# Down weights loaded as pairs of neighbouring rows per partition, activations transposed with a stride of two

## The chip, the core and the metric

The kernel runs on one core of one Trainium2 chip. A time is the device time of one execution in microseconds (us). The kernel before was timed in three runs: median 1532.12 us, from 1531.06 to 1533.81.

## The reference

A two-layer decoder trunk on 256 tokens of width 1024, in float32. The parts that the change touches are the two feed-forward blocks; both are SwiGLU, and the second one is applied once per expert with a gate per token.

```
# layer 0: x += diff_attention(rmsnorm(x));  x += swiglu(rmsnorm(x), wg, wu, wd)      (D_FF = 2816)
# layer 1: x += rglru_block(rmsnorm(x));     x += moe_swiglu(rmsnorm(x), ...)         (8 experts, top 2, D_FF_EXPERT = 3584)
def swiglu(t, wg, wu, wd):
    return (jax.nn.silu(t @ wg) * (t @ wu)) @ wd

def moe_swiglu(h, router, wg, wu, wd):
    ...
    for e in range(N_EXPERTS):
        out = out + comb[:, e:e + 1].astype(t.dtype) * swiglu(t, wg[e], wu[e], wd[e])
```

In `t @ wd` the contraction runs over the hidden width (2816 or 3584). The result does not depend on the order in which the hidden columns are taken, as long as activation and weight take the same one.

## The kernel before

All weights go through one stream of pieces of 1 MB (128 partitions x 2048 floats). SyncE issues them in program order (`load`, L312 to L316). Each landing slot is written again only after the piece that lay in it has been worked off: ring of 4 slots (`w_ring`) up to the experts, of 7 (three more in `work`) for the experts. For each piece ScalarE writes a rounded copy `w_hi` (L396), VectorE the remainder `w_lo` = piece - `w_hi` (L696, in the experts L1071), and TensorE multiplies with both: three fp32r matmuls (hi x hi, lo x hi, hi x lo) for each tile (`mm3`, L1157). `w_hi` and `w_lo` have 4 slots, freed by TensorE (`piece_used`).

The dense FFN works in chunks of 512 hidden columns (five, and one of 256), the experts in 7 chunks of 512. A chunk is gate, up, silu x up, a transpose of the activation by TensorE, and the product with the down weights one chunk later. A gate or up piece (`cols4`) has 4 runs of 512 floats per partition, which is 2 KB each. A down piece is 256 rows of the down weight: in the dense FFN `rows2` puts row r0 + p and row r0 + 128 + p on partition p, two runs of 4 KB; in the experts the view `md` does the same. The activation is turned in blocks of 128 neighbouring columns: `turn_chunk` (L1327) turns 4 blocks for each of two token blocks, `turn_e` (L1474) turns 4 blocks. In such a transpose the activation block is the stationary operand (loaded by LDWEIGHTS, engine PEld) and the identity the moving one. Block s, partition p then holds hidden column 128 s + p, and meets weight half s of the piece.

One expert pass is 42 pieces: 28 of gate and up, 14 of down. For each such piece TensorE runs 12 matmuls of 512 columns, in the dense FFN 24. The profiled execution made 8 passes. Its order of work is written out by hand for every engine, and nothing is scheduled by costs. At the end of a pass TensorE gathers the tokens of the next expert (L1428) and, at the start of the next, scatters the results (L1437, L1438).

Of the kernel before, what the change touches and what calls it, by code (L numbers as in the profile page):

```python
# [2 lines left out]

# [13 lines left out]
P = 128  # L29
# [11 lines left out]
def build_trunk(nc, x, norm_mix, norm_ffn, norm_final, rel_bias, w_qkv, w_o, lq1, lk1, lq2, lk2, subln,  # L41
# [16 lines left out]
    CW = 512  # L58
    EC = FE // CW
    FC = FF // CW  # L60
# [8 lines left out]
    def cols4(w, half, c0):  # L69
        return w.rearrange("(c p) n -> p c n", p=P)[:, 4 * half:4 * half + 4, c0:c0 + 512]  # L70

    def cols8(w, c0):
        return w.rearrange("(c p) n -> p c n", p=P)[:, :, c0:c0 + 256]

    def rows2(w, r0):
        return w[r0:r0 + 256, :].rearrange("(s p) n -> p s n", p=P)

    static = []
    wq = w_qkv[0]
    for part in range(2):  # L80
# [6 lines left out]
    fg, fu, fd = f_gate[0], f_up[0], f_down[0]  # L87
    for i in range(FC):
        static += [cols4(fg, h, CW * i) for h in range(2)]
        if i:  # L90
            static += [rows2(fd, CW * (i - 1) + 256 * h) for h in range(2)]
        static += [cols4(fu, h, CW * i) for h in range(2)]
    static += [cols8(fg, CW * FC)] + [rows2(fd, CW * (FC - 1) + 256 * h) for h in range(2)]
    static += [cols8(fu, CW * FC), rows2(fd, CW * FC)]

    def f_gate_at(i):
        return P_FFN + (0 if i == 0 else 6 * i - 2)
# [32 lines left out]
    def half_slot(n):  # L130
        return HALF[(n - P_MOE) % PASS]
# [3 lines left out]

    mg = m_gate.rearrange("a e (c p) f -> (a e) p c f", p=P)
    mu = m_up.rearrange("a e (c p) f -> (a e) p c f", p=P)
    md = m_down.rearrange("a e (s p) n -> (a e) p s n", p=P)

    def expert_pieces(e):  # L140
        pieces = []
        for i in range(EC):
            pieces += [mg[e, :, 4 * h:4 * h + 4, CW * i:CW * i + CW] for h in range(2)]
            pieces += [mu[e, :, 4 * h:4 * h + 4, CW * i:CW * i + CW] for h in range(2)]
            if i:
                pieces += [md[e, :, 4 * (i - 1) + 2 * h:4 * (i - 1) + 2 * h + 2, :] for h in range(2)]
        pieces += [md[e, :, 4 * (EC - 1) + 2 * h:4 * (EC - 1) + 2 * h + 2, :] for h in range(2)]
        return pieces

    def at(i):  # L150
        return 0 if i == 0 else 4 + 6 * (i - 1)
# [3 lines left out]
    with ExitStack() as ctx:  # L155
        def sb(name, shape, dt=F32):
            return ctx.enter_context(nc.sbuf_tensor(name, shape, dt))
# [14 lines left out]
        ident = sb("ident", [P, P])  # L172
# [56 lines left out]
        act_f = work[:, 0:1024].rearrange("p (b n) -> p b n", b=NB)  # L229
# [16 lines left out]
        act_e = work[:, 0:512]  # L246
# [19 lines left out]
        ps = ctx.enter_context(nc.psum_tensor("ps", [P, 8, 512], F32))  # L266
        GB, UB, TB, SB_, M0, M1, D0, D1 = range(8)
# [881 lines left out]
        def _(pe):  # L1149
            T = nc.tensor  # L1150

            def mm3(acc, xh, xl, wh, wl, start, stop, weights_stay=False):

                terms = ((xh, wh), (xl, wh), (xh, wl))
                for k, (a, b) in enumerate(terms):
                    stationary, moving = (b, a) if weights_stay else (a, b)
                    ins = T.matmul(acc, stationary, moving, start=start and k == 0, stop=stop and k == 2)  # L1157
                return ins
# [100 lines left out]
            for k in range(4):  # L1259
                ins = T.matmul(ps[:, 4 + k, :], flip, bias_up[:, 512 * k:512 * k + 512], start=True, stop=True)  # L1260
# [59 lines left out]
            transpose_hn(range(4), 0, norm=1)  # L1320
            pe.wait_ge(xt_lo_ok, 10)

            def turn_chunk(i, subs):
                for b in range(NB):
                    pe.wait_ge(fa, 2 * i + b + 1)
                    for s in range(subs):
                        ins = T.transpose(ps[:, 2 + b, P * s:P * s + P], act_f[:, b, P * s:P * s + P], ident[:, :])  # L1327
                    ins.then_inc(ft, 1)

            def narrow(n, banks):  # L1330
# [74 lines left out]
            for b in range(NB):  # L1405
                for c in range(KC):
                    ins = T.matmul(ps[:, M0, E * b:E * b + E], xtf[:, c, P * b:P * b + P], rw[:, c, :],
                                   start=c == 0, stop=c == KC - 1)
# [23 lines left out]
            def scatter():  # L1432

                for k, bank in enumerate((M0, M1, SB_, TB)):
                    b, half = divmod(k, 2)
                    o = slice(512 * half, 512 * half + 512)
                    T.matmul(ps[:, bank, :], onehotT[:, P * b:P * b + P], y_hi[:, o], start=True, stop=False)  # L1437
                    T.matmul(ps[:, bank, :], onehotT[:, P * b:P * b + P], y_lo[:, o], start=False,  # L1438
                             stop=True).then_inc(sc_ps, 1)
# [8 lines left out]
            def expert(p):  # L1448
                def slot(j):
                    n = P_MOE + j  # L1450
                    pe.wait_ge(lo_ready, p * PASS + (n + 1))
                    return w_hi[:, half_slot(n), :], w_lo[:, half_slot(n), :]

                def up_or_gate(j, bank, half):
                    wh, wl = (w.rearrange("p (c n) -> p c n", c=4) for w in slot(j))
                    for c in range(4):
                        ins = mm3(ps[:, bank, :], xt_hi[:, 4 * half + c, 0:P], xt_lo[:, 4 * half + c, 0:P],
                                  wh[:, c, :], wl[:, c, :], half == 0 and c == 0, half == 1 and c == 3)
                    ins.then_inc(piece_used, 1)

                def down_e(j, i, h):
                    wh, wl = (w.rearrange("p (s n) -> p s n", s=2) for w in slot(j))
                    for s in range(2):
                        for half, bank in enumerate((D0, D1)):
                            o = slice(512 * half, 512 * half + 512)
                            ins = mm3(ps[:, bank, :], eT_hi[i % 2][:, 2 * h + s, :], eT_lo[i % 2][:, 2 * h + s, :],
                                      wh[:, s, o], wl[:, s, o], (i, h, s) == (0, 0, 0), (i, h, s) == (EC - 1, 1, 1))
                    ins.then_inc(piece_used, 1)

                def turn_e(i):  # L1470
                    pe.wait_ge(ea_ok, p * EC + (i + 2))
                    pe.wait_ge(el_ok, p * EC + (i + 1))
                    for s in range(4):
                        ins = T.transpose(ps[:, TB, P * s:P * s + P], act_e[:, P * s:P * s + P], ident[:, :])  # L1474
                    ins.then_inc(et_ps, 1)

                for i in range(EC):
                    g0 = at(i)
                    pe.wait_ge(es_ok, p * EC + (i + 1))
                    if i == 0:  # L1480
                        pe.wait_ge(gat_hi, p * 2 + 2)
                        pe.wait_ge(gat_lo, p * 2 + 2)
                    up_or_gate(g0, GB, 0)
                    up_or_gate(g0 + 1, GB, 1)
                    if i == 0:
                        pe.wait_ge(ys_lo, p + 1)
                        pe.wait_ge(oht_ok, p + 1)
                        pe.wait_ge(el_ok, p * EC + 1)
                        scatter()
                    else:  # L1490
                        if i == 1:
                            pe.wait_ge(sc_ok, p * 4 + 4)
                            pe.wait_ge(oh_ok, p * 2 + 2)
                        turn_e(i - 1)
                        if i == 1:
                            for b in range(NB):
                                ins = T.transpose(ps[:, SB_, P * b:P * b + P], onehot[:, b, :].bitcast(F32), ident[:, :])
                            ins.then_inc(oht_ps, 1)
                    pe.wait_ge(ea_ok, p * EC + (i + 1))
                    up_or_gate(g0 + 2, UB, 0)  # L1500
                    up_or_gate(g0 + 3, UB, 1)
                    if i == EC - 1:
                        pe.wait_ge(oh_ok, p * 2 + 4)
                        pe.wait_ge(oht_ok, p + 2)
                        pe.wait_ge(es_ok, p * EC + (EC + 1))
                        gather(range(4))
                    if i:
                        pe.wait_ge(el_ok, p * EC + (i + 1))
                        down_e(g0 + 4, i - 1, 0)
                        if i == EC - 1:  # L1510
                            turn_e(i)
                        down_e(g0 + 5, i - 1, 1)
                pe.wait_ge(el_ok, p * EC + (EC + 1))
                down_e(PASS - 2, EC - 1, 0)
                down_e(PASS - 1, EC - 1, 1)
# [37 lines left out]
```

## Time and profile before

| | before |
|---|---|
| median of three runs | 1532.12 us |
| profiled execution, span | 1531.7 us |
| TensorE matmul busy | 1452.7 us (95%) |
| VectorE busy | 1164.9 us (76%) |
| ScalarE busy | 938.2 us (61%) |
| DMA, whole span | 427.41 MB in 193388 packets |

The span runs from the first to the last instruction of the core in the profiled execution; the page gives no other time of it. PE is the matmul side of TensorE and PEld its weight load; they overlap. A matmul's record contains its latency, so single records overlap and their means are longer than the pace at which they follow each other. The pace is read from the chain of waits. The expert passes lie between about 500 and 1520 us.

### The profile page before, as it was taken

What the parts mean: (1) busy time and instruction counts of PE and PEld (TensorE: products, weight loads), DVE (VectorE), ACT (ScalarE), POOL (GpSimd) and SP (SyncE); (2) the same over time, 40 slices, a digit from 0 to 9 for tenths busy, and PEclk for the clock granted to TensorE, in tenths of its full rate; (3) what the DMA queues carried; (4) which work ended last, traced back from release to release, by engine and by line L of the source; (5) the groups of instructions that cost most, each with busy time, mean ns of one, the idle gap of its engine ahead of it and who ended that gap; (6) DMA issues with size and microseconds to landing.
All of it is one profiled execution on the core that took longest, in us unless ns stands there. A gap on an engine that the chain in (4) does not pass through costs nothing.

```text
span 1531.7 us, 19136 instructions
## 1 busy us (share of the span) xinstructions
PE 1452.7 (95%) x7099; PEld 1215.4 (79%) x7099; DVE 1164.9 (76%) x1047; ACT 938.2 (61%) x778; POOL 11.6 (1%) x30
## 2 busy tenths in 40 slices
PE   5988999999989999999999999999999999999996
PEld 5877788888977778778878877877887887787785
DVE  5667444537675899888879788887888978888786
ACT  4554434434843677667667667766776766776674
POOL 3000000000000000000000000000000000000000
PEclk9998999999998999999999999999999999999999
DMA  9434345662462899899899989989989998998991
GB/s 280 154 110 155 127 172 192 210 222 84 151 242 86 304 335 369 313 352 370 316 333 387 342 329 351 362 313 340 365 311 350 385 344 328 350 363 310 337 370 48
DMA packets 193388, 427.41 MB, mean 279 GB/s; under 512 B 6921, under 2 KB 30049, under 8 KB 193345
## 3 DMA queue, kind: packets, MB, share of 16 engines
q1 hardware_dynamic: 192560, 425.49, 76.6%
q0 software_dynamic: 784, 1.33, 0.5%
q8 instruction: 29, 0.48, 0.1%
q14 instruction: 15, 0.11, 0.0%
HBM read 425.73 MB, written 1.06 MB: 279 GB/s over the span
## 4 chain that ended last, share of the span: by engine, by line
PE 83%; DVE 10%; issue 3%; ACT 3%; DMA 1%; DVEq 0%; SPq 0%; ACTq 0%
PE ps L1157 76%; DVE w_lo L1071 5%; PE ps L1428 2%; PE ps L1474 1%; ACT w_hi L396 1%; DVE w_lo L696 1%; DMA w_ring<-in_attn_w_qkv_dram 1%; PE ps L1211 1%; DVE hn L716 1%; PE ps L1437 1%; PE ps L1438 1%; DVE xres L782 0%; PE ps L1377 0%; DVE work L952 0%; DVE xt_lo L1076 0%
## 5 line engine op out<-in xcount | busy, mean ns | idle before, releaser
L396 ACT ACTIVATE w_hi<-w_ring 128x2048 fp32r<-128x2048 f32 x256 | 486.3, 1915 | 234.4 <-PE ps L1157 224.1
L1157 PE MATMUL ps<-w_hi,xt_hi 128*128 128x512 f32 (+1 forms) x1344 | 535.4, 398 | 28.7 <-DVE xt_lo L1076 18.3
L1157 PE MATMUL ps<-w_lo,xt_hi 128*128 128x512 f32 (+1 forms) x1344 | 525.7, 391 | 0.0
L1157 PE MATMUL ps<-w_hi,xt_lo 128*128 128x512 f32 (+1 forms) x1344 | 525.5, 391 | 0.0
L1071 DVE TENSOR_TENSOR w_lo<-w_ring,w_hi 128x2048 fp32r<-128x2048 f32 x191 | 432.3, 2286 | 65.4 <-ACT w_hi L396 65.0
L1071 DVE TENSOR_TENSOR w_lo<-work,w_hi 128x2048 fp32r<-128x2048 f32 x141 | 320.3, 2287 | 50.1 <-ACT w_hi L396 50.1
L396 ACT ACTIVATE w_hi<-work 128x2048 fp32r<-128x2048 f32 x144 | 275.2, 1917 | 108.8 <-PE ps L1157 108.4
L1157 PEld LDWEIGHTS ps<-w_hi,xt_hi 128*128 128x128 f32 x1344 | 255.7, 190 | 86.1 <-DVE w_lo L1071 25.1
L1157 PEld LDWEIGHTS ps<-w_lo,xt_hi 128*128 128x128 f32 x1344 | 255.9, 190 | 54.2
L1157 PEld LDWEIGHTS ps<-w_hi,xt_lo 128*128 128x128 f32 x1344 | 256.4, 191 | 50.3 <-issue 0.2
L1157 PE MATMUL ps<-w_hi,split 128*128 128x512 f32 x768 | 239.1, 393 | 9.2 <-DVE split L962 4.1
L696 DVE TENSOR_TENSOR w_lo<-w_ring,w_hi 128x2048 fp32r<-128x2048 f32 x65 | 148.1, 2287 | 65.2 <-ACT w_hi L396 65.1
L1157 PEld LDWEIGHTS ps<-w_hi,split 128*128 128x128 f32 x768 | 143.8, 189 | 43.1 <-DVE w_lo L1071 5.2
L1157 PE MATMUL ps<-w_lo,split 128*128 128x512 f32 x384 | 150.0, 390 | 0.0
L396 ACT ACTIVATE split<-ps 128x512 fp32r<-128x512 f32 (+2 forms) x53 | 34.1, 653 | 113.4 <-PE ps L1327 50.0
L1157 PE MATMUL ps<-xt_hi,w_hi 128*128 128x256 f32 x288 | 84.4, 293 | 7.7 <-DVE xt_lo L722 4.9
L1157 PEld LDWEIGHTS ps<-w_lo,split 128*128 128x128 f32 x384 | 72.4, 189 | 15.4
L1157 PE MATMUL ps<-xt_lo,w_hi 128*128 128x256 f32 x288 | 82.6, 287 | 0.0
L1157 PE MATMUL ps<-xt_hi,w_lo 128*128 128x256 f32 x288 | 82.5, 287 | 0.0
L1157 PEld LDWEIGHTS ps<-xt_hi,w_hi 128*128 128x128 f32 x288 | 56.4, 196 | 8.8 <-DVE xt_lo L722 4.2
L1157 PEld LDWEIGHTS ps<-xt_lo,w_hi 128*128 128x128 f32 x288 | 56.5, 196 | 0.1
L1157 PEld LDWEIGHTS ps<-xt_hi,w_lo 128*128 128x128 f32 x288 | 56.4, 196 | 0.0
(226 smaller groups left out, 808.7 us busy)
## 6 DMA issues: line engine op xcount, KB each, us to landing
w_ring<-in_moe_w_up_dram SPq DMA_DIRECT2D x72, 1024.0 KB, 7.0
w_ring<-in_moe_w_down_dram SPq DMA_DIRECT2D x72, 1024.0 KB, 7.1
work<-in_moe_w_gate_dram SPq DMA_DIRECT2D x64, 1024.0 KB, 6.5
w_ring<-in_moe_w_gate_dram SPq DMA_DIRECT2D x48, 1024.0 KB, 7.2
work<-in_moe_w_up_dram SPq DMA_DIRECT2D x40, 1024.0 KB, 7.0
work<-in_moe_w_down_dram SPq DMA_DIRECT2D x40, 1024.0 KB, 6.6
w_ring<-in_attn_w_qkv_dram SPq DMA_DIRECT2D x12, 1024.0 KB, 6.5
w_ring<-in_ffn_w_gate_dram SPq DMA_DIRECT2D x11, 1024.0 KB, 5.1
```

The lines of the kernel that those rows point to most:

```text
L396: return nc.scalar.activation(out, in_, ACT.Copy)
L696: V.tensor_tensor(w_lo[:, half_slot(k), :], land(k), w_hi[:, half_slot(k), :].bitcast(F32), ALU.subtract).then_inc(lo_ready, 1)
L716: V.scalar_tensor_tensor(hn[:, b, :], xres[:, b, :], rstd[:, b:b + 1], gain[:, :], ALU.mult, ALU.mult).then_inc(hn_ready, 1)
L1071: V.tensor_tensor(w_lo[:, half_slot(n), :], land(n), w_hi[:, half_slot(n), :].bitcast(F32), ALU.subtract).then_inc(lo_ready, 1)
L1157: ins = T.matmul(acc, stationary, moving, start=start and k == 0, stop=stop and k == 2)
L1211: T.matmul(ps[:, bank, :], xt_hi[:, 0, 0:P], xt_hi[:, 0:2, :], start=True, stop=True)
L1428: ins = T.matmul(ps[:, bank, P * m:P * m + P], h[:, b, P * c:P * c + P], onehot[:, b, :], start=b == 0, stop=b == NB - 1)
L1437: T.matmul(ps[:, bank, :], onehotT[:, P * b:P * b + P], y_hi[:, o], start=True, stop=False)
L1438: T.matmul(ps[:, bank, :], onehotT[:, P * b:P * b + P], y_lo[:, o], start=False, stop=True).then_inc(sc_ps, 1)
L1474: ins = T.transpose(ps[:, TB, P * s:P * s + P], act_e[:, P * s:P * s + P], ident[:, :])
```

## The change

Two views of the weights and two address patterns of the transposes are changed together.

- `pairs` takes the place of `rows2` for the dense down weights, and `md` is viewed with the pair innermost: partition p now holds rows r0 + 2p and r0 + 2p + 1, which lie next to each other in memory. A piece is the same 256 rows, the same 1 MB, in one run of 8 KB per partition. `w_out` of the recurrent block keeps `rows2`.
- `every_other` picks the columns of the activation for a transpose: of each 256 columns the even ones for the first block, the odd ones for the second. The stationary operand is so read with a step of two floats.

The number of instructions on every engine, their order and their waits stay as they are; so do slots, matmuls and all other operands. On SyncE's queue the down loads change their shape from 128x2x1024 to 128x2048.

```
+    def pairs(w, r0):
+        return w[r0:r0 + 256, :].rearrange("(p s) n -> p s n", p=P)
...
-            static += [rows2(fd, CW * (i - 1) + 256 * h) for h in range(2)]
+            static += [pairs(fd, CW * (i - 1) + 256 * h) for h in range(2)]
...
-    md = m_down.rearrange("a e (s p) n -> (a e) p s n", p=P)
+    md = m_down.rearrange("a e (q p s) n -> (a e) q p s n", p=P, s=2)
...
-                pieces += [md[e, :, 4 * (i - 1) + 2 * h:4 * (i - 1) + 2 * h + 2, :] for h in range(2)]
+                pieces += [md[e, 2 * (i - 1) + h] for h in range(2)]
...
+            def every_other(a, s):
+                o = 256 * (s // 2)
+                return a[:, o:o + 256].rearrange("p (t s) -> p s t", s=2)[:, s % 2, :]
...
-                        ins = T.transpose(ps[:, 2 + b, P * s:P * s + P], act_f[:, b, P * s:P * s + P], ident[:, :])
+                        ins = T.transpose(ps[:, 2 + b, P * s:P * s + P], every_other(act_f[:, b, :], s), ident[:, :])
...
-                        ins = T.transpose(ps[:, TB, P * s:P * s + P], act_e[:, P * s:P * s + P], ident[:, :])
+                        ins = T.transpose(ps[:, TB, P * s:P * s + P], every_other(act_e, s), ident[:, :])
```

## Rows read from the trace of the kernel before

**Rows 1.** The chain that ended last: share by engine, of the whole span.
```profile
PE 83%; DVE 10%; issue 3%; ACT 3%; DMA 1%; DVEq 0%; SPq 0%; ACTq 0%
```

**Rows 2.** Chain of waits, three pieces of 900 to 1050 us: start, length.
```profile
...
951.21 16.35 PE ps L1157 x72
967.56 0.44 PE ps L1474 x4
...
```

**Rows 3.** Chain of waits in the dense FFN.
```profile
...
257.53 32.68 PE ps L1157 x144
290.20 0.88 PE ps L1327 x8
...
```

**Rows 4.** Waits, whole span, those ended by a DMA: us, times, longest.
```profile
...
ACT w_hi L396 <- DMA w_ring<-in_attn_w_qkv_dram: 10.3, 5, 5.5
POOL work L380 <- DMA rel_scratch<-work: 4.3, 1, 4.3
ACT hn L419 <- DMA xres<-in_x_dram: 2.8, 2, 2.0
DVE hn L716 <- DMA gain<-in_norm_mix_dram: 0.2, 1, 0.2
```

**Rows 5.** Waits between 560 and 1500 us, largest of ACT, DVE, PEld and SP.
```profile
ACT w_hi L396 <- PE ps L1157: 237.5, 225, 4.9
...
DVE w_lo L1071 <- ACT w_hi L396: 110.5, 110, 3.9
...
PEld ps L1157 <- DVE w_lo L1071: 29.7, 21, 2.7
...
SPq L316 <- DVE w_lo L1071: 752.9, 307, 6.3
```

**Rows 6.** Windows: us, busy PE, PEld, DVE, ACT, POOL, PEclk, DMA share, GB/s.
```profile
520.00:1520.00 1000.00, 974.21 (x4479) 802.53 (x4478) 846.31 (x558) 683.81 (x460) 0.00 (x0) 0.99 0.92 337
...
903.26:1030.42 127.16, 124.20 (x574) 102.34 (x574) 108.58 (x69) 88.14 (x60) 0.00 (x0) 1.00 0.94 345
...
1080.00:1090.00 10.00, 10.00 (x45) 8.26 (x45) 9.08 (x6) 8.11 (x6) 0.00 (x0) 1.00 1.03 392
```

**Rows 7.** Loads of the expert down weights: ns min/median/max on SP; then us to landing.
```profile
L316 SPq DMA_DIRECT2D w_ring<-in_moe_w_down_dram x72: 372/373/373, 530.4 to 1489.8; - x72
...
DMA to landing us min/median/max: 4.8/7.0/8.9
```

**Rows 8.** Time order, SP, ACT and DVE around 1063 us: one down piece.
```profile
1063.01 2.43 SPq L316 DMA_DIRECT2D w_ring<-in_moe_w_down_dram  x2
...
1056.14 8.89 DVE L1071 TENSOR_TENSOR w_lo<-w_ring,w_hi 128x2048 fp32r<-128x2048 f32 x4 [3.56 <-ACT w_hi L396]
...
1076.86 1.92 ACT L396 ACTIVATE w_hi<-w_ring 128x2048 fp32r<-128x2048 f32 x1 [0.80 <-PE ps L1157]
...
1078.81 2.29 DVE L1071 TENSOR_TENSOR w_lo<-w_ring,w_hi 128x2048 fp32r<-128x2048 f32 x1 [0.42 <-ACT w_hi L396]
```

**Rows 9.** DMA of 520 to 1520 us: packets, then all issues of that line.
```profile
DMA packets 141668, 337.02 MB, mean 337 GB/s; under 512 B 5153, under 2 KB 5153, under 8 KB 141653
...
w_ring<-in_moe_w_down_dram SPq DMA_DIRECT2D x72, 1024.0 KB, 7.1
w_ring<-in_moe_w_up_dram SPq DMA_DIRECT2D x68, 1024.0 KB, 7.0
```

**Rows 10.** Weight loads by line: busy us, mean ns, idle before.
```profile
L1474 PEld LDWEIGHTS ps<-ident,work 128*128 128x128 f32 x224 | 27.7, 139 | 7.3
...
L1327 PEld LDWEIGHTS ps<-ident,work 128*128 128x128 f32 x44 | 5.0, 141 | 1.4 <-DVE work L897 0.7
...
L1241 PEld LDWEIGHTS ps<-work 128*128 128x128 f32 x16 | 2.7, 209 | 0.0
```

**Rows 11.** The w_lo and w_hi instructions of the experts: ns min/median/max.
```profile
L1071 DVE TENSOR_TENSOR w_lo<-w_ring,w_hi x191: 2272/2284/2294, 502.3 to 1505.0; 128x2048 fp32r<-128x2048 f32 x191
...
L396 ACT ACTIVATE w_hi<-w_ring x256: 1896/1918/1947, 13.2 to 1502.2; 128x2048 fp32r<-128x2048 f32 x128
```

More of the change, by code:

```diff
@@ L90, in build_trunk @@
         if i:
-            static += [rows2(fd, CW * (i - 1) + 256 * h) for h in range(2)]
+            static += [pairs(fd, CW * (i - 1) + 256 * h) for h in range(2)]
         static += [cols4(fu, h, CW * i) for h in range(2)]
-    static += [cols8(fg, CW * FC)] + [rows2(fd, CW * (FC - 1) + 256 * h) for h in range(2)]
-    static += [cols8(fu, CW * FC), rows2(fd, CW * FC)]
+    static += [cols8(fg, CW * FC)] + [pairs(fd, CW * (FC - 1) + 256 * h) for h in range(2)]
+    static += [cols8(fu, CW * FC), pairs(fd, CW * FC)]
     def f_gate_at(i):
@@ L145, in expert_pieces @@
             if i:
-                pieces += [md[e, :, 4 * (i - 1) + 2 * h:4 * (i - 1) + 2 * h + 2, :] for h in range(2)]
-        pieces += [md[e, :, 4 * (EC - 1) + 2 * h:4 * (EC - 1) + 2 * h + 2, :] for h in range(2)]
+                pieces += [md[e, 2 * (i - 1) + h] for h in range(2)]
+        pieces += [md[e, 2 * (EC - 1) + h] for h in range(2)]
         return pieces
```

## Prediction

> **What bounds the kernel now.** I read the chain that ended last first: 83% of it is TensorE, 10% VectorE, 1% DMA [rows 1]. So an edit counts if it changes TensorE's own work, or something that TensorE comes to wait for. In time order the chain shows what a stretch without trouble looks like: 72 matmuls of 512 columns in 16.35 us, then the four transposes of one chunk in 0.44 us, then matmuls again [rows 2]. That is 0.227 us a matmul and 12 x 0.227 = 2.72 us an expert piece. The dense FFN has the same pace: 144 matmuls in 32.68 us, then the 8 transposes of a chunk in 0.88 us [rows 3]. The transposes thus stand on the path itself, between matmuls, with nothing beside them that would hide a longer one.
>
> The loads are the other thing that is changed. The windows make them look near a limit: in a stretch in which TensorE runs without a gap the DMA engines are wholly busy at 392 GB/s, and over one expert pass they are at 0.94 with 345 GB/s [rows 6]. But the list of waits tells whether anybody waits for them. In the whole span a DMA ended waits of 10.3, 4.3, 2.8 and 0.2 us, every one of them in the attention stage or at the start [rows 4]. None is for a down piece. In the experts each engine waits for another: ScalarE for TensorE to free a slot (237.5 us), VectorE for ScalarE (110.5), the weight load for VectorE (29.7), and SyncE for VectorE to free a landing slot (752.9) [rows 5]. The kernel is slow at the far end of the chain from the DMA.
>
> **Part one, the loads.** 14 x 8 = 112 expert pieces and 11 dense ones change from two runs of 4 KB per partition to one of 8 KB. The number of loads, their bytes and SyncE's 0.373 us for each issue [rows 7] need not change. The packet counts show that a run is a packet here. The 337.02 MB between 520 and 1520 us are 321 pieces of 1.049 MB; a gate or up piece would be 128 x 4 packets, a down piece 128 x 2, each with 16 small ones for completion. By the mix of a pass, (28 x 528 + 14 x 272) / 42 = 443 packets a piece, 321 pieces make 142,000, and the row has 141,668; the 5153 small ones are 321 x 16 and a few [rows 9]. So 123 x 128 = 15,744 packets should go, of 193,388.
>
> What is that worth? I take it from the cover of a single piece. The load at 1063.01 is let go by the third of the four remainders of the row that starts at 1056.14, which ends at 1065.03 - 2.22 = 1062.81. It is for the piece seven places later, whose `w_hi` starts at 1076.86, after ScalarE has waited 0.80 us for TensorE, and not for the load, and whose `w_lo` starts at 1078.81 [rows 8]. A landing takes 7.0 us in the median and 8.9 at worst [rows 7], so the piece lies there for 1076.86 - 1063.01 - 7.0 = 6.8 us before anybody touches it, 4.9 us with the worst landing. A faster landing only makes that longer: worth 0. A slower one costs nothing until a landing takes 13.8 us, nearly twice as long. In the dense FFN the ring has 4 slots, and a piece takes 24 x 0.227 = 5.45 us, so a load has some 4 x 5.45 = 21.8 us less the work on it. The lower bound of this part (a gain) is what quieter transfers could give the engines that share the memory with them: `w_lo` takes 2272 ns at its fastest and 2284 in the median [rows 11], so 332 remainders could win at most 332 x 12 ns = 4 us if all stood on the path. VectorE has a tenth of it, so 0.4 us. The upper bound is in the rivals. I take 0.
>
> **Part two, the transposes.** 8 x 7 x 4 = 224 in the experts and 5 x 8 + 4 = 44 in the dense FFN, 268 in all; each has now a stationary operand whose columns lie 8 bytes apart in place of 4. Today they cost 224 x 0.44 / 4 + 44 x 0.88 / 8 = 24.6 + 4.8 = 29.4 us of the path [rows 2, 3]. That 0.11 us a transpose is a pace of the weight load rather than of the stream: the moving side is 128 columns, a quarter of a matmul that takes 0.227 us, so 0.057 us. Whatever a stepped read adds to the load is therefore added to the path. No row shows a weight load with a step. Bounds: at the lower end nothing, since the number of columns (128), the bytes and the instruction are the same, and no reason speaks for a gain. At the upper end each load takes twice its time: + 0.11 us x 268 = + 29.4 us. Between them, a load as long in its record as the slowest one with 128 columns, 209 ns against 139 [rows 10], would add 0.07 x 268 = 18.8 us. The row nearest is that of the same instruction on the same tile, 139 ns, so I take 0 and keep the 29.4 for the range.
>
> A rule bears on this. The Trainium skill, page "SBUF — State Buffer", section "Door 1: The DMA port swizzle", says that the memory is read in lines of 16 bytes and keeps full rate while at least two accesses fall in each line. A step of two floats leaves exactly two. By the rule the sum is 0; were every new line to cost as such, twice as many lines would make it the doubling priced above. No row here has a stepped read of TensorE, so the trace neither bears the rule out nor speaks against it.
>
> **The sum.** Span 1531.7 + 0 (loads) + 0 (transposes) = 1531.7 us. The median of the runs is 1532.12, 0.4 us above the span, which I keep: 1532.1 us. The runs shown spread from 1531.06 to 1533.81, so about 0.2% (3 us) is what a measurement of this kernel can tell from no change.
>
> **The rivals.**
> - *A stepped weight load is slower (slower kernel).* Place: the groups of transposes, 56 in the experts and 6 in the dense FFN. Price: 29.4 us with doubled loads, 1561.5 us; the first load of each group could hide behind the last matmul before it (0.227 us), which leaves 3 of 4, + 22 us, 1554 us. It decides from + 0.012 us a transpose (3 us over 268). For it: nothing lies beside these loads, and the 0.11 us is their own pace. Against: same columns, same bytes; a step this small is the mildest there is.
> - *The 8 KB runs land more slowly, and the DMA becomes the bound (slower).* For it: share 1.03 at 392 GB/s [rows 6] says that there is no room in a clean stretch, and the 14 down pieces are a third of the traffic. Against: a down piece with 4 KB runs lands in 7.1 us, one of 2 KB runs in 7.0 [rows 9], so the length of a run hardly tells. Price: a pass has 0.06 x 127 = 7.6 us of DMA time to spare [rows 6]. If a down piece kept the engines 50% longer, 14 x 0.5 x 2.7 = 19 us a pass, 11 us would stay uncovered, x 8 = 90 us: 1622 us. It decides from 7.6 / (14 x 2.7), about + 20% a down piece.
> - *Lighter DMA traffic speeds something up (faster).* For it: 15,744 packets fewer where the engines are full. Against: rows 4 and 5, no wait for a landing, and the 0.4 us above. To show it would have to bring 3 us, all of it from the 29.7 us in which the weight load waits for `w_lo`, a wait for VectorE's own 2.28 us an instruction. Price if it took a sixth of that off: - 5 us, 1527 us.
> - *The change does not do what it says:* the runs of 8 KB are cut into two of 4 KB again. Then the packets stay at 193,388, and the time is that of my forecast.
>
> **How the numbers follow.** Forecast, with the last rival inside it: 0.77. Slower weight load: 0.14. DMA as the bound: 0.02. Faster: 0.07. The likeliest case alone is 1529.5 to 1534.5 us. The range has to reach into the slower weight load, whose price is unknown between 3 and 29 us; to 1545 us it holds its lower part (up to 0.05 us a transpose), and down to 1529 the near edge of the faster case: 1529 to 1545 us, with about 0.8 inside. Faster by over 0.2%: 0.07, within 0.2%: 0.77, slower by over 0.2%: 0.14 + 0.02 = 0.16.
>
> **What the profile after would show.** Packets down from 193,388 to about 177,600, with the count under 8 KB down further. The four transposes of a chunk at 0.44 us in the chain and 139 ns a weight load on L1474's successor: above 0.5 us the slower case is there, and every 0.1 us of it is 5.6 us of time in the experts. No wait ended by a load of down weights. Landing of a down piece between 6 and 8 us; the other loads may land a little sooner, with nobody the better for it. The same granted clock of 0.99 in the experts. I would be wrong in the forecast's reason, even with a fitting time, if the transposes grew and something else shrank by as much.

## The result, and the profile after

| | before | changed |
|---|---|---|
| median, runs | 1532.12 us, 13 | 1535.81 us, 13 |
| lowest and highest | 1527.47, 1533.83 | 1532.36, 1540.08 |
| profiled execution: span | 1531.7 | 1535.3 (its time: 1537.11) |

The ratio to before is 1.0027, with a 95% interval of 1.0018 to 1.0037: slower by 2.8 to 5.7 us, in the middle 4.1; the two medians lie 3.7 us apart. The forecast was no change; it had priced the stepped transposes at nothing. The other half of the change came as forecast, so I begin with that. The packets of the whole run, then those between 520 and 1520 us, to be held against [rows 9]:

```profile
DMA packets 177643, 427.41 MB, mean 278 GB/s; under 512 B 6920, under 2 KB 30048, under 8 KB 161856
```

```profile
DMA packets 127752, 336.99 MB, mean 337 GB/s; under 512 B 5154, under 2 KB 5154, under 8 KB 113826
```

15,745 packets are gone. Of those that remain 15,787 are of 8 KB or more, where there were 43: the runs of 8 KB are real. What they brought is a shorter issue (345 against 373 ns) and a landing 0.1 us earlier; columns as in [rows 7], of the changed kernel:

```profile
L307 SPq DMA_DIRECT2D w_ring<-in_moe_w_down_dram x72: 332/345/346, 530.3 to 1493.3; - x72
...
DMA to landing us min/median/max: 4.7/6.9/8.7
```

The engines wait for each other as in [rows 5], and no wait ends with a down weight. The largest waits between 560 and 1500 us of the changed kernel (in total, times, longest):

```profile
ACT w_hi L387 <- PE ps L1148: 240.3, 223, 4.9
...
DVE w_lo L1062 <- ACT w_hi L387: 113.3, 111, 3.9
...
PEld ps L1148 <- DVE w_lo L1062: 29.4, 21, 2.7
...
SPq L307 <- DVE w_lo L1062: 758.4, 307, 6.5
```

The transposes did change. Their weight loads, to be held against [rows 10] (busy us, mean ns, idle before):

```profile
L1469 PEld LDWEIGHTS ps<-ident,work 128*128 128x128 f32 x224 | 35.4, 202 | 4.4
...
L1322 PEld LDWEIGHTS ps<-ident,work 128*128 128x128 f32 x44 | 6.1, 206 | 1.0 <-DVE work L888 0.7
```

A load with a step of two lasts 202 ns in its record and not 139. Most of this is only longer overlap with its neighbours. The chain tells what reaches the path, as [rows 2] and [rows 3] did (start, length):

```profile
953.15 0.47 PE ps L1469 x4
953.62 16.38 PE ps L1148 x72
...
```

```profile
257.29 32.70 PE ps L1148 x144
289.99 0.95 PE ps L1322 x8
```

Four transposes take 0.47 us where they took 0.44, eight take 0.95 where they took 0.88. The 72 matmuls read 16.35 to 16.44 us in the two kernels from group to group, so a whole expert pass is the better ruler. The chain has in every pass a stretch of 48 matmuls behind a wait (the first of each pair below), and another one some 19 us later. Of the kernel before:

```profile
1030.54 11.19 PE ps L1157 x48
1049.92 12.81 PE ps L1157 x48
1159.31 11.17 PE ps L1157 x48
1178.67 11.17 PE ps L1157 x48
1286.45 11.19 PE ps L1157 x48
```

Of the changed kernel:

```profile
1033.09 11.18 PE ps L1148 x48
1052.52 11.17 PE ps L1148 x48
1160.50 11.20 PE ps L1148 x48
1179.94 12.79 PE ps L1148 x48
1289.55 11.18 PE ps L1148 x48
```

From pair to pair there are two lengths of a pass in each kernel. Where the second stretch takes 11.2 us, a pass takes 127.14 us before (1159.31 to 1286.45) and 127.41 after (1033.09 to 1160.50). Where it takes 12.8, a pass takes 128.77 and 129.05. So there are two differences side by side in these two executions. One is there in every pass: 0.26 us over the seven groups of transposes, 8 x 0.26 = 2.1 us in the experts, and 0.5 us in the dense FFN, which lasts 184.1 us against 183.6, so 2.6 us together. The other is a slow stretch of 48 matmuls, + 1.6 us, in some passes (I call it a drop): four of eight in the trace before, five of eight in the one after. Together 2.6 + 1.6 = 4.2 us, less 0.5 us by which this execution was earlier at the end of the attention stage: 3.7, and the spans differ by 3.6. This accounts for the two profiled executions; on the other executions see "What stays open" further down.

The slow stretch is the clock. Windows around it, of the kernel before (columns as in [rows 6]), with a slow one first:

```profile
1045.00:1061.00 16.00, 13.71 (x54) 10.81 (x53) 10.55 (x7) 11.11 (x8) 0.00 (x0) 0.89 0.75 265
1173.00:1189.00 16.00, 13.71 (x60) 11.01 (x60) 11.02 (x7) 11.96 (x8) 0.00 (x0) 1.00 0.86 305
```

TensorE is idle for 2.3 us in both, in the third chunk of each pass, where it waits for the remainder of the turned activation. After it the granted clock is 1.00 (2.4 GHz throughout) in the one and 0.89 in the other, a mean of stretches at 2.4 and at 1.2 GHz.

### The profile page after: what moved, and what is told of

Read it like the earlier page. It is cut to its first block, busy times and chain, and to the rows that moved or that the text cites. A ratio compares the mean times of both kernels' runs of the same rounds, so it can differ in the third digit from the quotient of the medians.

```text
span 1535.3 us, 19136 instructions
## 1 busy us (share of the span) xinstructions
PE 1455.5 (95%) x7099; PEld 1220.7 (80%) x7099; DVE 1165.0 (76%) x1047; ACT 938.3 (61%) x778; POOL 12.1 (1%) x30
## 2 busy tenths in 40 slices
DMA packets 177643, 427.41 MB, mean 278 GB/s; under 512 B 6920, under 2 KB 30048, under 8 KB 161856
## 4 chain that ended last, share of the span: by engine, by line
PE 81%; DVE 10%; issue 3%; ACT 3%; DMA 1%; DVEq 0%; SPq 0%; POOL 0%; ACTq 0%; POOLq 0%
PE ps L1148 74%; DVE w_lo L1062 5%; PE ps L1423 2%; PE ps L1469 1%; ACT w_hi L387 1%; DMA w_ring<-in_attn_w_qkv_dram 1%; DVE w_lo L687 1%; PE ps L1202 1%; DVE hn L707 1%; PE ps L1432 1%; PE ps L1433 0%; DVE xres L773 0%; DMA work<-rel_scratch 0%; PE ps L1372 0%; DVE work L943 0%
## 5 line engine op out<-in xcount | busy, mean ns | idle before, releaser
L1148 PE MATMUL ps<-w_hi,xt_hi 128*128 128x512 f32 (+1 forms) x1344 | 535.8, 399 | 28.7 <-DVE xt_lo L1067 18.3
```

## The experiments

Theory A was that the step in the weight load is the whole cause, theory B the loads of the weights, theory C that mere shifts of timing change how often the clock drops. Ratios are to the kernel before, on the same chip in the same rounds. The experiments e1 to e4, e5 to e8 and e9 to e12 each shared a chip, on which the kernel before had medians of 1532.55, 1531.95 and 1531.20 us. e1, e2, e7 and e8 leave out the matching of weight rows to activation columns; this changes values, not the instructions or their waits, and their traces show 8 expert passes too.

**e1, the 8 KB loads alone.** The transposes go back to neighbouring columns, here and in the dense FFN (`...` stands for lines left out).

```
...
-                        ins = T.transpose(ps[:, TB, P * s:P * s + P], every_other(act_e, s), ident[:, :])
+                        ins = T.transpose(ps[:, TB, P * s:P * s + P], act_e[:, P * s:P * s + P], ident[:, :])
```

> Down weights as pairs of rows (8 KB runs), transposes contiguous as before; rows and activation columns are so matched wrongly, which costs no time of its own. Theory A (the stepped weight load costs, the loads are free): as before, 1532 us, within 0.1%; 177,640 packets; transposes at 0.44 us in the chain, 139 ns a weight load. Theory B (the new loads cost, by landings or contention): about 1536 us, as the changed kernel. Theory C (the difference is only how often the clock drops at the handover between experts, which any change of timing reshuffles): anything from 1530 to 1537.

Measured: 1531.46 us, ratio 0.9993 (0.9983 to 1.0004). 177,643 packets, weight load 139 ns, passes of 127.16 us, drops in four of eight. The loads are worth nothing: by the interval they cost at most 0.04% and win at most 0.2%. Theory B falls.

**e2, the step alone.** Loads as before, here and in the dense FFN.

```
...
-    md = m_down.rearrange("a e (q p s) n -> (a e) q p s n", p=P, s=2)
+    md = m_down.rearrange("a e (q s p) n -> (a e) q p s n", p=P, s=2)
```

> Loads as before (two runs of 4 KB), transposes with a step of two; rows and columns matched wrongly. Theory A: 1535 us, 0.15 to 0.3% above before; weight load of the transposes 202 ns, an expert pass without a clock drop 127.41 us against 127.16. Theory B: 1532 us. Theory C: pass lengths as under A, but the time anywhere from 1532 to 1538, by the number of drops.

Measured: 1536.88 us, ratio 1.0021 (1.0009 to 1.0033), the change's own within the intervals. Weight load 202 ns, passes of 127.4 us (129.0 with a drop), drops in five of eight.

**e3, a step of four.**

```
+    def quads(w, r0, h):
+        return w[r0:r0 + 512, :].rearrange("(p s) n -> p s n", p=P)[:, 2 * h:2 * h + 2, :]
...
+            def every_fourth(a, s):
+                return a.rearrange("p (t s) -> p s t", s=4)[:, s, :]
```

> Chunks of 512 hidden columns dealt out by fours: each down piece holds two of four neighbouring rows per partition (8 KB runs), transposes read every fourth column, 16 bytes apart. If a stepped load only starts later (latency, once a group): same as the change, a pass of 127.4 us, about 1535 us. If each new memory line costs: more per transpose, 0.05 to 0.11 us x 268 = 13 to 29 us over before, 1545 to 1561 us.

Measured: 1535.96 us, ratio 1.0023 (1.0010 to 1.0037). The same groups in the chain, and the same load, as with a step of two:

```profile
709.51 0.47 PE ps L1475 x4
709.98 16.38 PE ps L1151 x72
```

```profile
L1475 PEld LDWEIGHTS ps<-ident,work 128*128 128x128 f32 x224 | 35.6, 203 | 4.0
```

The passes are 127.4 us, with a drop in four of eight. 16 bytes between columns cost what 8 do. Of the steps tried (two and four) the price is for having one at all; larger ones were not run.

**e4, the step in the evacuation of PSUM.** 8 KB loads kept, transposes of neighbouring columns; silu and the product with up read every other column instead.

```
-                nc.scalar.activation(act_e, ps[:, GB, :], ACT.Silu).then_inc(es_ok, 1)
+                nc.scalar.activation(blocks(act_e), pair_up(ps[:, GB, :]), ACT.Silu).then_inc(es_ok, 1)
...
-                V.tensor_tensor(act_e, act_e, ps[:, UB, :], ALU.mult).then_inc(ea_ok, 1)
+                V.tensor_tensor(blocks(act_e), blocks(act_e), pair_up(ps[:, UB, :]), ALU.mult).then_inc(ea_ok, 1)
```

> 8 KB loads; the step of two is taken out of the transposes and put where silu and the product with up read PSUM (ScalarE 0.59 us, VectorE 0.68 us each). If PSUM is read with a step at full rate: transposes back at 139 ns, 1532 us as before. If those reads slow down to twice their time: + 0.6 us for each chunk on ScalarE and VectorE, hidden in most chunks, but not where the chain runs over them (once a pass, and VectorE's lag at the start of a pass): + 1.2 us x 8 = 10 us, 1542 us.

Measured: 1533.20 us, ratio 1.0002 (0.9992 to 1.0012). The step costs these two engines nothing; silu and the product (ns min/median/max) took 578/589/600 and 670/679/689 before, and here:

```profile
L637 ACT ACTIVATE work<-ps x56: 579/588/598, 498.6 to 1497.4; 128x512 f32<-128x512 f32 x56
```

```profile
L1079 DVE TENSOR_TENSOR work<-work,ps x56: 668/681/689, 505.3 to 1503.3; 128x512 f32<-128x512 f32 x56
```

So the pairing of rows can be had without its price, within the interval of 0.1% either way. It has no gain either.

**e5 and e6, filling the standstill, in the wrong place.** Before and changed kernel, at the end of each pass:

```
                 down_e(PASS - 1, EC - 1, 1)
+                for _ in range(10):
+                    T.matmul(ps[:, UB, 0:P], ident[:, :], ident[:, :], start=True, stop=True)
```

> Kernel before, with 10 small fp32 matmuls (identity x identity, 128 columns, into a free bank) in the 2.3 us in which TensorE stands still at each handover between experts; their output is used by nobody. If that standstill is what lets the clock drop at about every second handover (1.6 us each, 4 of 8 in the trace): all passes at 127.2 us, time 4 x 1.6 = 6 us less, 1526 us, and less scatter between runs. If the drops come from something else: 1532 us as before, or a little more if the 10 matmuls last longer than the gap.

> The same 10 matmuls in the changed kernel. Theory A alone (latency of the stepped load, 0.26 us a pass and 0.5 us in the dense FFN): 2.6 us above e5, 0.17%. If the change also made drops of the clock more frequent (5 against 4, theory C), the distance without drops is 2.6 us and the rest of the 4.1 us is gone; if the whole 4.1 us is the load's own, the distance stays at 4.1 us.

Measured: 1544.46 us, ratio 1.0085 (1.0072 to 1.0098), and 1543.40 us, ratio 1.0080 (1.0064 to 1.0096). I had taken the 2.3 us for a gap between experts. They lie in the third chunk, and stayed there, 18.3 us in eight waits in either. At the end of a pass TensorE has no such gap, and the 10 matmuls (each float32 matmul stands in the trace as two) were added to the path:

```profile
1006.58 2.23 PE ps L1517 x20
```

Seven of the eight groups cost this. The last one ran in TensorE's wait before the final scatter, which shrank from 2.7 to 0.4 us. 7 x 2.23 = 15.6 us, of which drops won some back: two of eight are left in e5, none in e6, though the standstill of 2.3 us was still there in both. So the standstill alone does not bring a drop. Something else decides as well, and what it is stays open. The distance between the two (-1.1 us, five and six runs) tells nothing against intervals of 0.13 to 0.16%.

**e7 and e8, which of the four transposes.** The step in the first only, and in the other three only.

```
...
-                        ins = T.transpose(ps[:, TB, P * s:P * s + P], every_other(act_e, s), ident[:, :])
+                        ins = T.transpose(ps[:, TB, P * s:P * s + P], every_other(act_e, s) if s == 0 else act_e[:, P * s:P * s + P], ident[:, :])
```

In e8 the condition is `s > 0`.

> Change with the step in the first transpose of each group of four only; the other three are contiguous, and rows and columns are matched wrongly. If the price is a longer start of a load that shows only where the queue of loads begins: nearly all of the 0.26 us a pass stays if the first load carries it, none if it is seen at the end of the group. If it is a pace, a quarter: 0.07 us a pass, 127.23 us.

> The complement of e7: step in the second to fourth transpose, first one contiguous. Pace: three quarters, 127.36 us a pass. Latency at the group's start: none, 127.16 us. Latency at its end (the last transpose ends later and with it the release of the next load or of the split): all of it, 127.42 us.

Measured: e7 1532.99 us, ratio 1.0002 (0.9991 to 1.0013), passes of 127.18 us. e8 1535.73 us, ratio 1.0025 (1.0013 to 1.0036), passes of 127.37 us. A group in the chain takes 0.44 us in e7 and 0.47 in e8. The first load of a group is free within 0.04 us a pass, though its record grows to 200 ns. That it is hidden because it runs beside the last matmul of 0.227 us is my reading of it. The other three carry it, about 0.01 us each. That leaves a pace (shown from the second load on) and a price at the group's end, which e11 and e12 part.

**e9 and e10, the standstill filled where it is.** Before and changed kernel:

```
+                    if i == 2:
+                        for _ in range(9):
+                            T.matmul(ps[:, M0, 0:P], ident[:, :], ident[:, :], start=True, stop=True)
                     if i:
                         pe.wait_ge(el_ok, p * EC + (i + 1))
                         down_e(g0 + 4, i - 1, 0)
```

> Kernel before, with 9 fp32 matmuls (identity x identity, 128 columns, 0.22 us each as e5 showed) into a free bank in the standstill of 2.3 us that every pass has in its third chunk, before the down product (e5 and e6 had them at the end of the pass, where TensorE was not idle, and they cost 2.2 us a pass). Right behind this standstill the slow 48 matmuls of 12.8 us stand. If it is what lets the clock drop: all eight passes at 127.2 us, no stretch of 12.8 us, 4 x 1.6 = 6.4 us less, 1526 us. If the drops have another cause: about 1532 us, drops as before.

> The same in the changed kernel. If the load's latency is the whole of its price: all passes at 127.4 us and 2.6 us (0.17%) above e9, 1528.5 us. If the drops of the clock gave the rest of the measured 4 us (5 of 8 against 4 of 8), that rest is gone here; if the distance to e9 is still 4 us, something in the step costs that the passes do not show.

Measured: e9 1525.17 us, ratio 0.9959 (0.9945 to 0.9972), the fastest version of all. e10 1528.06 us, ratio 0.9980 (0.9969 to 0.9991). In time order, TensorE of e9 at the former standstill (idle time before it in brackets); it was 2.29 us:

```profile
1044.67 2.17 PE L1509 MATMUL ps<-ident 128*128 128x128 f32 x18
1047.12 0.49 PE L1157 MATMUL ps<-w_hi,xt_hi 128*128 128x512 f32 x1 [0.27 <-DVE xt_lo L1076]
```

The stretches of 48 matmuls in its chain, and in that of e10:

```profile
1027.73 11.17 PE ps L1157 x48
1047.12 11.16 PE ps L1157 x48
1154.86 11.17 PE ps L1157 x48
...
```

```profile
1026.51 11.18 PE ps L1148 x48
1045.93 11.16 PE ps L1148 x48
1153.91 11.18 PE ps L1148 x48
...
```

None of the sixteen passes of the two has a slow stretch. Passes take 127.13 us in e9 and 127.40 in e10: with the drops away, the step's own price is left. The medians lie 2.9 us apart where 2.6 were expected. With intervals of 0.11 to 0.14% either way this fits 2.6, but would not exclude 4. In e10's profiled execution the clock did fall once, behind the last pass, in the final scatter (windows of e9, then of e10, columns as in [rows 6]):

```profile
1513.00:1517.00 4.00, 2.10 (x8) 1.42 (x8) 2.98 (x6) 1.71 (x4) 0.00 (x0) 1.00 0.00 0
```

```profile
1513.00:1517.00 4.00, 3.52 (x8) 2.51 (x8) 2.28 (x5) 1.02 (x3) 0.00 (x0) 0.57 0.00 0
```

**e11 and e12, sixteen transposes in place of four.** Before and changed kernel, in the experts; e12 with `every_other`:

```
+                    for _ in range(3):
+                        for s in range(4):
+                            T.transpose(ps[:, TB, P * s:P * s + P], act_e[:, P * s:P * s + P], ident[:, :])
                     for s in range(4):
```

> Kernel before, every group of four transposes in the experts done four times over (16 in place of 4, the same blocks into the same places; the reference for e12). 12 x 56 = 672 more at 0.11 us: + 74 us, 1606 us; the chain shows 16 transposes in 1.76 us.

> The changed kernel with the same 16 in place of 4, all with the step of two. Latency (a stepped load is 63 ns longer, its pace the same): as far from e11 as the change is from before, 0.26 us a pass, 2 to 4 us. Pace (each transpose 9 ns slower, 0.26 / 28): four times the price, 1.0 us a pass, 8 to 9 us above e11.

Measured: 1600.56 us, ratio 1.0455 (1.0438 to 1.0472), and 1606.56 us, ratio 1.0491 (1.0475 to 1.0507), 6.0 us apart. One group in the chain of each, e11 first:

```profile
996.75 1.31 PE ps L1475 x12
998.06 0.44 PE ps L1477 x4
```

```profile
1000.50 1.43 PE ps L1470 x12
1001.93 0.48 PE ps L1472 x4
```

1.91 us against 1.75: 0.16 us for 16, 0.010 us each, and not 0.03 once. It is a pace. Passes without a drop take 136.90 us against 135.66, 1.24 us more, nearly five times the 0.26 of four transposes, as 15 to 3 loads behind a first one (0.012 us each in both). That is 8 x 1.24 + 0.5 = 10.4 us. The measured distance is smaller, 6.0 us between the medians, which lies between the two forecasts (2 to 4 and 8 to 9); it is the pass lengths that decide for the pace. The spans of the two profiled executions differ by 7.0. There e12 had two drops where e11 had four (- 3.2 us), and only e11 ran the final scatter slowly (about 1 us): this time the clock hid a part of the step. Whether it did so in the other executions (four of each kernel in all) no trace shows.

## Why the prediction was wrong

- **The sentence that failed** is "I take 0", for the transposes. The bounds were + 0 and + 29.4 us, and I went by the row of the same instruction with neighbouring columns. The step has a price, near the low end: about 0.012 us for each transpose but the first of a group. In the experts that is 8 x 0.26 = 2.1 us, in the dense FFN 0.5 us: a term of 2.6 us in place of 0, or 0.010 us over all 268. The rival I had written for this named its place. Its tipping point was close (3 us over 268 is 0.011; I wrote 0.012), but I had given it 0.14 and priced it at 22 and 29.4 us. The mechanism was priced as all or nothing, where a tenth of a transpose was enough to be seen.
- **A sign I had set too high.** I wrote that the slower case is there above 0.5 us a group. It was there at 0.47. With 62 groups on the path, 0.03 us a group is 1.9 us, already more than half of the 3 us that I took as what can be told.
- **The load's record is no price.** I had worked out 18.8 us from a record of 209 instead of 139 ns. The record did grow to 202 to 206 ns, but the 63 ns overlap with the neighbouring instructions, and the path took 10 to 12. The argument that a longer load has no cover within a group was right, from the second transpose on: e11 and e12 show the price multiply.
- **The rule.** The Trainium skill, page "SBUF — State Buffer", section "Door 1: The DMA port swizzle", says that full rate holds while two accesses fall in a line of 16 bytes. By it a step of two floats is free and one of four, with one access in a line, is not. (The same note then gives 4 float32 as how far one can stride for free; by that sentence neither would cost.) The runs show another thing: both cost the same 0.01 us (e2, e3). Here the measurement decides. My lean on 0 agreed with that sentence, and it did not hold for this weight load.
- **The loads: right in all parts.** 15,745 packets fewer (said: 15,744), no wait for them, landings of 6.9 us (said: 6 to 8), and e1 at 0.9993. The one miss is without a price: the issue fell from 373 to 345 ns.
- **The clock: not seen.** I looked at the granted clock of the whole expert stage, 0.99 [rows 6], and passed over what makes it less than one: drops of 1.6 us in about half of the passes. They are not all of the scatter between runs. Twelve runs of e10, whose trace has no drop in the experts, still spread over 6.8 us. And in the profiled executions with four transposes a group the first stretch of 48 matmuls starts anywhere from 515.0 us (e5) to 520.0 (e2), so up to 5 us arise ahead of it. Whether the step made drops more frequent is open. The profiled executions with all four, or three, transposes stepped had 5, 5, 4 and 4 of eight (changed kernel, e2, e3, e8); those with none or one had 4 each (before, e1, e4, e7). Half a drop is 0.8 us, which would take 2.6 to 3.4 us, inside the interval of the result; 2.6 alone lies just under its lower end of 2.8, and inside those of e2 and e3.
- **What stays open.** The step's own 2.6 us is shown; the rest of the 4.1 us is not explained. The single times say that it is no even shift. Of the 49 executions of the four stepped kernels (changed, e2, e3, e8) 25 took 1536.4 us or more, 21 took 1534.5 or less, and only three lie between. None of the 123 executions of kernels without the step, or with it in the first transpose alone (before, e1, e4, e7), took more than 1535.6 us. The profiled executions in the upper group (changed, e2) had five drops and reached the first stretch of 48 at 518.6 and 520.0 us, those in the lower one (e3, e8) four drops, at 516.1 and 516.7. One drop is 1.6 us of this distance, and the rest arose ahead of the experts. Why the stepped kernels fall into two groups no run shows.

## What to carry to other kernels

When a change makes each transfer's runs longer, first look whether any wait ends with that transfer; DMA engines at a share of 1.0 were no bound here, with 6.8 us between landing and use. A step in TensorE's stationary operand has a small price a piece, so count the pieces on the path; if a permutation is needed, put it where ScalarE and VectorE read PSUM, which was free. In a kernel bound by TensorE look for repeated standstills of a few us and for slow matmuls behind them: filling one that costs 2.3 us anyway won 0.4% (e9). Fill only time in which the engine really waits: ten matmuls in a place without a wait cost 0.8% (e5, e6).

## What the runs showed of the hardware

- A weight load of 128 float32 columns with a step of 8 or 16 bytes: record 202 or 203 ns against 139, pace of transposes about 0.12 against 0.11 us (measured for the step of 8 bytes in e11 and e12; four transposes take 0.47 us with either step).
- ScalarE and VectorE read float32 of PSUM with a step of two in 588 and 681 ns, against 589 and 679.
- One run of 8 KB per partition in place of two of 4 KB: half the data packets, SyncE's issue 345 against 373 ns, landing 6.9 against 7.0 us, time the same.
- The same idle time of 2.3 us is followed by a drop of the granted clock (0.89 over 16 us, 1.6 us lost) in one pass and by none in the next. Of eight it was four or five. With the idle time filled to 0.27 us there was none at this place in two executions (e9, e10), and with it left but 2.2 us of matmuls more at the end of each pass two and none (e5, e6).
